# Column sums of the norms taken with the ones as weights, in four column groups, and turned by a transpose

## What is computed

```
y = xf * lax.rsqrt(jnp.mean(xf * xf, axis=-1, keepdims=True) + EPS)
```

## Time and profile before

| | |
|---|---|
| median of 3 runs | 1812.98 us (1812.31 to 1816.6) |
| the profiled execution | 1812.97 us |
| its span, first to last instruction | 1811.2 us |
| PE busy | 1799.5 us, 99% |
| weight loads on PE (overlap the matmuls) | 1456.2 us, 80% |
| DVE busy | 1039.3 us, 57% |
| ACT busy | 735.6 us, 41% |
| POOL busy | 48.6 us, 3% |
| mean granted TensorE clock | 0.998 |

### The profile page before, as it was taken

One profiled execution on the slowest core, in us unless ns is written; L12 is line 12 of the kernel. 1 busy time (PEld: TensorE's weight loads), 2 busy tenths in 40 slices (PEclk: granted clock), 3 DMA queues, 4 the chain that ended last, 5 costly groups with the idle time before them and its releaser, 6 DMA issues.

```text
span 1811.2 us, 21230 instructions
## 1 busy us (share of the span) xinstructions
PE 1799.5 (99%) x8390; PEld 1456.2 (80%) x8390; DVE 1039.3 (57%) x1502; ACT 735.6 (41%) x1202; POOL 48.6 (3%) x109
## 2 busy tenths in 40 slices
PE   9999999999999999999999999999999999999998
PEld 7777777888766788888888888888888888888887
DVE  8899986566687565444333356554444544444333
ACT  5788885433477532322222332223222322322221
POOL 1001011001210000000000000000000000000000
PEclk9999999999999999999999999999999999999999
DMA  5254442222211223223333323233233323333331
GB/s 181 80 106 112 118 99 96 98 96 91 70 36 36 82 81 105 93 93 101 93 100 102 117 82 94 94 98 99 94 100 98 94 93 103 95 93 94 104 97 56
DMA packets 63123, 170.86 MB, mean 94 GB/s; under 512 B 5808, under 2 KB 22704, under 8 KB 63024
## 3 DMA queue, kind: packets, MB, share of 16 engines
q1 hardware_dynamic: 62160, 168.78, 30.6%
q10 hardware_dynamic: 864, 0.72, 0.1%
HBM read 167.31 MB, written 2.16 MB: 94 GB/s over the span
## 4 chain that ended last, share of the span: by engine, by line
PE 94%; DVE 2%; ACT 2%; DMA 1%; issue 1%; DVEq 0%; SPq 0%; ACTq 0%
PE pb L788 28%; PE pb L790 28%; PE pb L789 28%; PE pb L1007 2%; PE pb L899 2%; PE pb L1036 1%; PE pb L1012 1%; PE pb L1180 1%; PE pb L1182 1%; PE pb L1181 1%; DMA DB<-cum 1%; PE pb L802 1%; ACT LL L1298 0%; ACT LL L1302 0%; PE pb L1190 0%
## 5 line engine op out<-in xcount | busy, mean ns | idle before, releaser
L788 PE MATMUL pb<-XR,wr 128*128 128x512 f32 x1584 | 625.6, 395 | 0.6 <-DVE wl L1586 0.5
L790 PE MATMUL pb<-XR,wl 128*128 128x512 f32 x1584 | 617.2, 390 | 0.0
L789 PE MATMUL pb<-XL,wr 128*128 128x512 f32 x1584 | 617.0, 390 | 0.0
L1586 DVE TENSOR_TENSOR wl<-raw,wr 128x1024 fp32r<-128x1024 f32 (+1 forms) x297 | 358.2, 1206 | 350.7 <-ACT wr L1238 349.5
L1238 ACT ACTIVATE wr<-raw 128x1024 fp32r<-128x1024 f32 (+1 forms) x295 | 305.3, 1035 | 298.6 <-PE pb L790 273.0
L788 PEld LDWEIGHTS pb<-XR,wr 128*128 128x128 f32 x1584 | 297.5, 188 | 65.6 <-issue 3.9
L790 PEld LDWEIGHTS pb<-XR,wl 128*128 128x128 f32 x1584 | 297.3, 188 | 62.7
L789 PEld LDWEIGHTS pb<-XL,wr 128*128 128x128 f32 x1584 | 297.7, 188 | 60.2 <-issue 0.2
L788 PE MATMUL pb<-ffn2HR,wr 128*128 128x512 f32 (+1 forms) x198 | 72.7, 367 | 0.0
L789 PE MATMUL pb<-ffn2HL,wr 128*128 128x512 f32 (+1 forms) x198 | 72.4, 366 | 0.0
L790 PE MATMUL pb<-ffn2HR,wl 128*128 128x512 f32 (+1 forms) x198 | 72.4, 365 | 0.0
(11 more groups left out here) (353 smaller groups left out, 2248.7 us busy)
## 6 DMA issues: line engine op xcount, KB each, us to landing
raw<-in_ffn_in SPq DMA_DIRECT2D x88, 512.0 KB, 3.5
raw<-in_mix_in SPq DMA_DIRECT2D x48, 512.0 KB, 3.4
raw<-in_ssm_in SPq DMA_DIRECT2D x40, 512.0 KB, 8.1
raw<-in_ffn_out SPq DMA_DIRECT2D x32, 512.0 KB, 3.5
DB<-cum SPq DMA_DIRECT2D x28, 256.0 KB, 8.7
raw<-in_ffn_out SPq DMA_DIRECT2D x16, 384.0 KB, 3.1
raw<-in_mla_in SPq DMA_DIRECT2D x11, 512.0 KB, 3.3
raw<-in_ssm_out_a SPq DMA_DIRECT2D x8, 512.0 KB, 3.3
```

The source lines that it names most:

```text
L788: e.matmul(o, r, xr, start=first, stop=False)
L789: e.matmul(o, r, xl, start=False, stop=False)
L790: return e.matmul(o, l, xr, start=False, stop=last)
L1586: e.tensor_tensor(wl[j % NS][:, 0:width(j)], raw[j % NR][:, 0:width(j)], wr[j % NS][:, 0:width(j)].bitcast(F32), ALU.subtract).then_inc(s_ ...
```

## The change

The sums are formed the other way round. A block of ones, 128 partitions by 32 columns, is the weight, and 128 tokens of the accumulator are the moving operand. The four blocks of tokens go to four groups of 32 output partitions, so the result stands as four rows of 128 tokens (each repeated 32 times). DVE copies these 128x128 values from PSUM into the new tile ST (`sums_out`), PE transposes ST (`turn_sums`), and DVE reads every 32nd column of the result (`columns`) where it read 4 columns before. "m" has two such results; the second goes by way of RS. The transpose stands one tile later than the sum for g0 to g2, one step later for x, g3 and mx, and at step 0 of the next tile for kv, ck, cq, m and f2. Two semaphores are new: `s_sumcp` (PE waits for the copy) and `s_sumt` (DVE waits for the transpose). The last norm is unchanged.

```diff
@@ planner, Mamba part
             if x[1][0] == "gsum":
+                due.append((no + 1, ("gturn", x[1][1])))
                 due.append((no + (5 if x[1][1] == 0 else 3), ("gscale", x[1][1])))
...
-    tile(36, [(6, ("xsum",))])
+    tile(36, [(6, ("xsum",)), (7, ("xturn",))])
...
-    tail = {0: [("gfold", 3)], 1: [x[1] for x in due] + [("gsum", 3)], 5: [("gscale", 3)]}
+    tail = {0: [("gfold", 3)], 1: [x[1] for x in due] + [("gsum", 3)], 2: [("gturn", 3)], 5: [("gscale", 3)]}
@@ PE
             for i in range(4):
-                m = e.matmul(o[:, at + i:at + i + 1], accs[key][:, 128 * i:128 * i + 128], ones[:, 0:1], start=True,
-                             stop=True)
+                m = e.matmul(o[32 * i:32 * i + 32, at:at + 128], ones[:, 0:32], accs[key][:, 128 * i:128 * i + 128],
+                             start=True, stop=True)
             m.then_inc(s_sums, 1)
+
+        def turn_sums(key, n=1):
+
+            o = PB[bk.bank["sum " + key]]
+            w.wait_ge(s_sumcp, turned[key])
+            for i in range(n):
+                m = e.transpose(o[:, 256 + 128 * i:384 + 128 * i], (RS if i else ST)[:, 0:128], ident[:, :])
+            m.then_inc(s_sumt, 1)
...
-            def side(i):
+            def side(i, t):
+                if t == 0 and i in (0, 3, 9):
+                    turn_sums({0: "kv", 3: "ck", 9: "cq"}[i])
+                if t != 7:
+                    return
...
+                if f == 0 and j == 2 and t == 0:
+                    turn_sums("m", 2)
+                if f == 1 and j == 1 and t == 0:
+                    turn_sums("f2")
...
                         if t == 6 and hf == 0:
                             sums("mx")
+                        if t == 7 and hf == 0:
+                            turn_sums("mx")
@@ DVE
+        def sums_out(key, n=1):
+
+            w.wait_ge(*bk.full["sum " + key])
+            o = PB[bk.bank["sum " + key]]
+            if n == 2:
+                e.tensor_copy(RS[:, 0:128], o[:, 128:256])
+            e.tensor_copy(ST[:, :], o[:, 0:128]).then_inc(s_sumcp, 1)
+
+        def columns(key, i=0):
+
+            w.wait_ge(s_sumt, turned[key])
+            return PB[bk.bank["sum " + key]][:, 256 + 128 * i:384 + 128 * i:32]
+
         def root(key, n=D):
-            w.wait_ge(*bk.full["sum " + key])
-            e.tensor_scalar(SV[:, :], PB[3][:, 0:4], 1.0 / n, EPS, ALU.mult, ALU.add).then_inc(s_sv, 1)
+            sums_out(key)
+            e.tensor_scalar(SV[:, :], columns(key), 1.0 / n, EPS, ALU.mult, ALU.add).then_inc(s_sv, 1)
...
             elif what == "gsum":
+                sums_out(f"g{m[0]}")
+            elif what == "gturn":
                 sum_of(f"g{m[0]}", 512)
...
                 if i == 2:
+                    sums_out("ck")
                     sum_of("ck", 256)
...
                 if i == 8:
+                    sums_out("cq")
                     sum_of("cq", 384)
```

More of the change, by code:

```diff
@@ L348, in build_in @@
     mneg = sb("mneg", [128, 128], BF16)
+    ST = sb("ST", [128, 128])
     SV, SS, RN, RQ, RT, RP, GV, GW, GN = [sb(n, [128, 4]) for n in ("SV", "SS", "RN", "RQ", "RT", "RP", "GV", "GW",
@@ L465, in build_in @@
     s_dww, s_dtraw, s_dtev, s_dtabs, s_dtexp, s_dt = [sem("s_dt" + n) for n in ("w", "raw", "ev", "abs", "exp", "")]
+    s_sumcp, s_sumt = sem("s_sumcp"), sem("s_sumt")
     s_nega, s_cum, s_prior, s_pv = sem("s_nega"), sem("s_cum"), sem("s_prior"), sem("s_pv")
@@ L515, in build_in @@
                                             "fin1"))}
+    turned = {n: i + 1 for i, n in enumerate(("x", "g0", "g1", "g2", "g3", "kv", "ck", "cq", "m", "mx", "f2"))}
     def whole(name, n):
@@ L832, in ssm_side @@
                 sums("x")
+            elif what == "xturn":
+                turn_sums("x")
             elif what == "xscale":
@@ L863, in ssm_side @@
                 sums(f"g{m[0]}")
+            elif what == "gturn":
+                turn_sums(f"g{m[0]}")
             elif what == "gscale":
@@ L961, in latents @@
             for i, n in enumerate(MLA_ORDER):
-                tile_of(("mi", n), "mla_in", n, XR, XL, ready=(s_xlo, 16), side=lambda t: side(i) if t == 7 else None)
+                tile_of(("mi", n), "mla_in", n, XR, XL, ready=(s_xlo, 16), side=lambda t: side(i, t))
             w.wait_ge(s_cklo, 2)
@@ L1084, in ffn, with side @@
             name = f"ffn{f + 1}"
-            def side(j):
+            def side(j, t):
+                if f == 0 and j == 2 and t == 0:
+                    turn_sums("m", 2)
+                if f == 1 and j == 1 and t == 0:
+                    turn_sums("f2")
+                if t != 7:
+                    return
                 if f == 0 and j == 1:
                     sums("m1", 0, "m")
-                    sums("m2", 4, "m")
+                    sums("m2", 128, "m")
                 if f == 0 and j == READY[0]:
@@ L1100, in ffn @@
                 tile_of((name, j % 2, j // 2), name + "_in", FT * (j % 2) + j // 2, XR, XL,
-                        ready=(s_xlo, 32 if f == 0 else 48), side=lambda t: side(j) if t == 7 else None)
+                        ready=(s_xlo, 32 if f == 0 else 48), side=lambda t: side(j, t))
             for c in range(KT if f == 0 else KT - 1):
@@ L1637, in sum_of @@
         def sum_of(key, n):
-            w.wait_ge(*bk.full["sum " + key])
             if key != "g0":
                 w.wait_ge(s_groot, rooted[key][1] - 1)
-            e.tensor_scalar(GV[:, :], PB[bk.bank["sum " + key]][:, 0:4], 1.0 / n, EPS, ALU.mult, ALU.add).then_inc(s_sv, 1)
+            e.tensor_scalar(GV[:, :], columns(key), 1.0 / n, EPS, ALU.mult, ALU.add).then_inc(s_sv, 1)
         def softplus():
@@ L2047, in ffn_side @@
             if f == 0 and j == 1:
-                w.wait_ge(s_sums, sums_no["m2"])
-                e.tensor_scalar(SV[:, :], PB[3][:, 0:4], 1.0 / D, EPS, ALU.mult, ALU.add).then_inc(s_sv, 1)
+                sums_out("m", 2)
+                e.tensor_scalar(SV[:, :], columns("m"), 1.0 / D, EPS, ALU.mult, ALU.add).then_inc(s_sv, 1)
                 w.wait_ge(s_sv, taken["m"])
@@ L2054, in ffn_side @@
                 w.wait_ge(c.h, c.n)
-                e.tensor_tensor(RP[:, :], RP[:, :], PB[3][:, 4:8], ALU.mult).then_inc(s_sv, 1)
+                e.tensor_tensor(RP[:, :], RP[:, :], columns("m", 1), ALU.mult).then_inc(s_sv, 1)
                 w.wait_ge(s_sv, taken["m2"])
```

## The result

| | before | after |
|---|---|---|
| median, us | 1812.99 (1812.31 to 1816.6, 4 runs) | 1822.82 (1821.78 to 1823.24, 4 runs) |
| ratio | | 1.0052, 95% interval 1.0039 to 1.0065 |
| profiled execution, us | 1812.97 | 1822.87 |
| its span, us | 1811.2 | 1821.1 |

By the medians the change costs 9.8 us, 0.54%, and the interval of the ratio lies wholly above 1; the forecast was 1821.3, with a range of 1816.5 to 1825.0.

The account below looks back on a forecast made before the run. TensorE (PE), busy 1799.5 of 1811.2 us, was taken as the bound. kv and ck +8.2, other sums -5.6, transposes +1.9, waits +1.5, clock +2.3: +8.3 on the profiled 1812.97 us gives 1821.3, range 1816.5 to 1825.

Parts of the forecast that it names:

- The stall at ck: At ck's transpose, tile 3 step 0: PE stands 6.7 us for DVE's copy, which comes from 425.1.
- kv: At kv's transpose: PE stands 2.5 us for DVE's late copy; the spread starts at 406.4 instead of 404.56.
- Together: kv and ck with their savings and transposes: +8.2 us, before the clock's separate charge of 2.3.
- The rival that the stall is partly absorbed: At ck: DVE gets to the copy some 3 us earlier than laid out, 1814 to 1818 us; chance 0.15.
- The rival that the groups don't overlap: At the twelve sums: the new form saves nothing, +6.1 us over ten sums, 1827 us; chance 0.03.
- The clock: Behind ck's wait: PE's granted clock falls after 6.7 us without a matmul, charged once with 2.3 us.
- a fall at kv as well: Clock also falls at kv's 2.5 us wait; part of the more-is-lost rival, 1823 to 1825 us, chance 0.17.
- The sum: At each sum: eight new instructions take 0.25 us instead of 0.81, saving 0.56; ten sums -5.6 us.
- The transpose: Twelve added on PE: 0.2 us each, 0.1 for m's second, bounds 0.17 and 0.36; +1.9 outside kv and ck.
- The small waits: PE waits at x 0.7, g2 0.4, g3 0.2 and m 0.2 us, +1.5; g0, g1, cq, mx and f2 lose nothing.

Follow-up runs that it names:

- e7: Changed kernel with x, g0 to g3, kv, cq, mx and f2 back in the old form, leaving ck and m new: 1820.89 us, ratio 1.0044.
- e1: Changed kernel with 26 spare float32 matmuls put on PE in front of its wait at ck: 1820.05 us, ratio 1.0042.
- e12: Changed kernel with DVE's copies at kv and ck moved up, and each sum's four matmuls issued twice: 1814.05 us, ratio 1.0007.
- e10: Changed kernel with DVE's copies at kv and ck, and ck's reading, moved up in DVE's queue; PE's order unchanged: 1812.21 us, ratio 0.9998.
- e2: Changed kernel with ck's transpose before step 7 of tile 3 in place of step 0: 1815.97 us, ratio 1.0017.
- e3: Changed kernel with ck's transpose before step 4 of tile 4 and DVE's reading at the start of iteration 3: 1814.39 us, ratio 1.0006.
- e4: Changed kernel with kv alone back in the old form, without copy or transpose: 1820.28 us, ratio 1.0042.

## Why the prediction was right

**The stall at ck** was right in place and size. DVE's copy was to come at 425.1 and came at 425.93, in an execution that was 0.94 us later from the start (g3's spread at 311.85 for 310.91): 1.5 us behind the kernel before, predicted 1.6. PE stood 6.41 us, predicted 6.7. That DVE's chain there is not paced by PE is shown by e7: with kv undone, and PE standing from 417.3 on, the copy started at 423.51, where the earlier trace rows put the read at 423.51.

**kv**: PE stood 2.18 us, predicted 2.5; the spread came 1.70 later than before, predicted 1.8.

**Together** they were to cost 8.2 and 2.3 for the clock, 10.5; measured 1.70 + 8.84 = 10.54. The rival that the stall is partly absorbed is refuted by the last rows of the table above: behind ck nothing is given back but the sums' own gains. The rival that the groups don't overlap is refuted by 0.35 us for eight instructions.

**The clock** was charged once with 2.3; e1 puts it at 2.5. That it fell was reasoned from rows; that the size fits within 0.2 is in part luck, since twelve slow matmuls cost 2.4 us (0.20 each) and the six of e7 only 1.2. The rule of the Trainium skill ("TensorE: Matmul & The Clock Gate", "Why this matters for your kernels") that idle gaps between bursts put the clock back is borne out: 0.50 behind the wait, 1.00 when spare matmuls fill it. What I had as a rival, a fall at kv as well, did not happen in the profiled execution, and did in three others with the same 2.18 us wait. How often it happens was not counted. Two of the four executions of the changed kernel have a mean clock of 0.995 in place of 0.997, which suggests more time at the low clock in them; they were not traced. That the forecast needed only one charge is therefore shown for one execution, and is luck as far as the others go.

**The terms that were mis-sized** cancel in part. The sum: "I take 0.25, since shape, type and groups are the same" left out that the row's 40 instructions share one fixed part, while each sum pays its own (e12): 0.09 at the entry (0.32 from the matmul before to the first of the eight, 0.23 is usual) and 0.10 more behind. At cq two matmuls that enclose the sum are 1.35 us apart before and 1.01 after, so a sum saves 0.34, not 0.56. The transpose: taken at 0.2, measured 0.11 (at cq the matmuls before and behind it are 0.57 apart, two pitches are 0.46); it was below my lower bound of 0.17, and no run shows why. Sum and transpose, net of each other: -0.23 a place where I had -0.36. At m, where two sums follow each other, the pair saves 1.02 (2.25 us to 1.23 between the matmuls round it) and the two transposes cost 0.25, close to what I had. Over the eight other places outside kv and ck that is 1.1 us less gain than I reckoned.

**The small waits**: x was to lose 0.4 and 0.3 and shows 0.15 (the transpose at 21.03, 0.38 behind a matmul at 20.65) and 0.4 at the spread (0.63 behind a matmul; the table's 0.2 is the idle part); g2 was to lose 0.4 at its spread and lost 0.5, 0.3 of it idle, waiting for GpSimd; m 0.2, shows 0.28; g3 0.2, shows none (its transpose at 303.55 keeps the pitch). Together 1.3, where I had 1.5. g0, g1, cq, mx and f2 wait for no copy, as said.

The forecast of 1821.3 is 1.5 us below the median. The gain that the sums don't give is 1.1 of it, less the 0.2 that the small waits fell short. The other 0.6 stays open: the stretch up to g0's spread alone differs by 0.9 between the two profiles, and a fall of the clock at kv in untraced executions would be in the median.

## What to carry to other kernels

Where one engine bounds the kernel, count what a change makes it wait for before counting what it saves: put its arrival at the new wait beside the time at which the other engine, by its own in-order queue, gets to the work. An operation of 0.28 us cost 8.8 us because it stood at the end of a busy queue, and almost nothing when it was moved up, at ck to where that queue had been idle. A sum over partitions, a read or a copy that nobody waited for becomes a synchronisation as soon as the bounding engine needs its result back. And when such a wait is unavoidable, its price for TensorE can be the wait and a slow stretch behind it: a fall of the clock was seen in all three profiles with a wait of over 6 us, and in three of the four with one of 2.2 us.

## What was not expected of the hardware

- The granted clock fell to 1.2 GHz after a wait of 2.18 us in three of four profiled executions with that wait (e1, e2 and e3, not the changed kernel), once when PE had been at work again for over a microsecond. Near 103 us it fell behind 1.99 us in e10's profile, and not behind 2.08 us in the changed kernel's or 1.71 us in that of the kernel before.
- Behind the wait of 6.4 to 6.6 us at ck, six, eight or twelve matmuls ran at the slow pitch of 0.43 us (e7, e4, the changed kernel).
- A float32 transpose of 128x128 between matmuls of 512 columns adds 0.11 us to PE's stream; four column groups of a float32 matmul of 128 columns cost 0.0275 us an instruction (0.22 for eight) and some 0.2 fixed for the group (0.09 ahead of the first, 0.13 behind the last).
